# Experts' rows added to x2 in memory by the scatter, and a finish that loads one row per token

## The chip, the cores and the metric

One core of one Trainium2 chip runs the whole kernel. The metric is the time of one execution on the device in microseconds (us); it is the median of several runs. A profiled execution is a run of its own, with its own time.

## What is computed

One layer of a decoder on 1024 tokens of 1024 float32 values: a token mixer of three branches, then a mixture of experts, then a last RMS norm. The change is in the last two steps. In the reference's terms:

```python
x = x + hybrid_mixer(rms_norm(x, norm1_w), ...)          # the kernel calls this x2
h = rms_norm(x, norm2_w)                                  # h2
x = x + hierarchical_moe(h, ...)
return rms_norm(x, final_norm_w)
# hierarchical_moe: each token goes to 2 of 32 experts (both of one group), with weights
hid = silu(xblk @ w_gate[e]) * (xblk @ w_up[e])           # [rows, 512]
y   = hid @ w_down[e]                                     # [rows, 1024]
out[token] = weight_1 * y_first + weight_2 * y_second
```

So the result's row for a token is the norm of three rows added: x2 and two experts' weighted outputs.

## The kernel before

The kernel is a series of blocks with a barrier of all engines between them. Each engine has its own list of instructions and waits on semaphores. Behind each block `semaphores.clear` (line 57) lets POOL clear the block's semaphores and sets another barrier (line 58), in which every engine drains its queue.

`merge_and_route` finishes the mixer, stores x2 and h2 to memory (`s_x`, `s_h` in the profile's names), picks two experts for each token and stores a table: for each expert up to 128 records per slab with the token's number (column 0), the number of the pair, token + pick * 1024 (column 1), and the weight (column 2).

`experts_first_slabs` runs the 32 experts, one slab of at most 128 rows each. For each expert, float32 products are done as three products of split values: ACT copies a piece of weights of 128 x 2048 to a rounded `hi` (L2655, L2665), DVE takes the rest `lo` (L2710, L2715), and PE multiplies hi*hi, hi*lo and lo*hi (L2782, L2767). Who does what:

- SP loads the weights of the next expert: four pieces for gate and up (L2578) and two for down (L2590), 1 MB each, each when DVE has read the buffer's last content. Each piece has one buffer.
- POOL gathers the rows of h2 for expert e+2 (L2622) and then scatters the weighted outputs of expert e-1 (L2630). Before, a row goes to `pairs`, a scratch of 2048 rows in memory, at the number of its pair, so that each row is written once and nothing is read. The two indirect transfers share POOL's queue.
- ACT weighs the output (`weigh`, L2672) into one of two buffers `ye`, then POOL may scatter it. ACT waits until the scatter two experts back has landed.
- At the end of the block SP loads x2 back into SBUF: five pieces of 128 rows into `x2_kept` (L2599) during the last expert but one, three into buffers of down weights (L2603) when these are free, and the last norm's weights (L2604). Then it waits for all scatters (L2607), loads `todo`, the list of further slabs (L2608), and the pairs of the first four pieces of tokens (L2610), 1 MB each.

`experts_further_slabs` handles experts with more than 128 rows. Each engine reads `todo` and skips everything if it is empty, as with these inputs. SP first loads the pairs of the last four pieces (L2861); POOL clears a buffer (L2877).

`finish` takes the eight pieces of 128 tokens in turn. For the pieces 0, 1, 4 and 7 DVE adds the two rows of a pair (L3003) and adds that to x2 (L3005). For the pieces 2, 3, 5 and 6 PE adds the two rows by products with the identity into PSUM (L2988), and DVE makes the second addition alone. ACT takes the sum of squares (L3025), Ln (L3026) and Exp (L3027), DVE scales with the norm's weights (L3009), and SP stores the piece (L2978). DVE scales piece c-1 after it has added piece c.

Of the kernel before, what the change touches and what calls it, by code (L numbers as in the profile page):

```python
# [8 lines left out]
F32 = mybir.dt.float32  # L9
# [1748 lines left out]
GK, DK = 2 * KT // GU, FF // P // DN  # L1758
KEPT = 5
AHEAD = 2  # L1760
# [738 lines left out]

def experts_first_slabs(nc, io, dr, ident, dn_raw, gu_raw, x2_kept, x2_tail, final_w, recs, recs_in, todo, todo_in, pairs, pairs_in,  # L2500
                        kept_sem):
# [10 lines left out]
    with ExitStack() as ctx:  # L2512
# [24 lines left out]
        dn_used = sem("dn_used")  # L2537
        x2_in = sem("x2_in")
        gathered = [kept_sem(f"gathered{b}") for b in range(2)]
# [29 lines left out]
        def _(sp):  # L2569
# [27 lines left out]
            experts(body)  # L2597
            for c, kept in enumerate(x2_kept):
                sp.dma_start(kept[:], dr["x2"][c * CH:(c + 1) * CH, :]).then_inc(x2_in, 16)  # L2599
            sp.wait_ge(dn_ready, DN * LAST)  # L2600
            for n, tail in enumerate(x2_tail):
                c = len(x2_kept) + n
                sp.dma_start(tail, dr["x2"][c * CH:(c + 1) * CH, :]).then_inc(x2_in, 16)  # L2603
            sp.dma_start(final_w, io["final_norm_w"].unsqueeze(0).to_broadcast([P, D])).then_inc(x2_in, 16)  # L2604
            sp.wait_ge(dn_used, DN * N_EXPERTS)
            for b in range(2):
                sp.wait_ge(scattered[b], 16 * N_EXPERTS // 2)  # L2607
            sp.dma_start(todo[:], dr["work"].rearrange("(o n) w -> o (n w)", o=1)).then_inc(todo_in, 16)  # L2608
            for c in range(GU):
                sp.dma_start(pairs[c], pair_rows(dr, c)).then_inc(pairs_in[c], 16)  # L2610
            sp.wait_ge(x2_in, 16 * (NCH + 1))

        @block.gpsimd
        def _(pool):
# [11 lines left out]
            def scatter(e, b, turn):  # L2626

                pool.wait_ge(y_ready, e + 1)
                pool.sem_inc(passed, 1)
                pool.indirect_dma_start(out=dr["pairs"], out_offset=bass.IndirectOffsetOnAxis(ap=recs[:, e, 1:2], axis=0),  # L2630
                                        in_=ye[b][:], in_offset=None, bounds_check=2 * T - 1, oob_is_err=False)\
                    .then_inc(scattered[b], 16)
# [166 lines left out]

def pair_rows(dr, c):  # L2800

    return dr["pairs"].rearrange("(a t) d -> t a d", a=2)[c * CH:(c + 1) * CH]


def experts_further_slabs(nc, io, dr, ident, todo, todo_in, pairs, pairs_in):

# [3 lines left out]
    with ExitStack() as ctx:  # L2810
# [47 lines left out]
        @block.sync  # L2858
        def _(sp):
            for c in range(GU, NCH):  # L2860
                sp.dma_start(pairs[c], pair_rows(dr, c)).then_inc(pairs_in[c], 16)  # L2861
            sp.sem_inc(slab_done, 1)

            def body(n, place, expert):

                sp.wait_ge(slab_done, n + 1)
                one = bass.ds(expert, 1)
                sp.dma_start(rec[:].unsqueeze(1), dr["table"].rearrange("(s e) w -> s e w", e=N_EXPERTS)[bass.ds(place, SLAB), one, :])\
                    .then_inc(rec_in, 16)
                for w, p in ((wg, 0), (wu, GU // 2), (wdn, GU)):  # L2870
                    sp.dma_start(w[:].rearrange("p k f -> p (k f)").rearrange("p (a m) -> p a m", a=2),
                                 io["moe"][one, p:p + 2].rearrange("o a p m -> p (o a) m")).then_inc(w_in, 16)
            slabs(sp, body)

        @block.gpsimd
        def _(pool):
# [3 lines left out]
            def body(n, place, expert):  # L2880
# [6 lines left out]
                pool.sem_inc(passed, 1)  # L2887
                pool.indirect_dma_start(out=dr["pairs"], out_offset=bass.IndirectOffsetOnAxis(ap=rec[:, 1:2], axis=0),
                                        in_=ye[:], in_offset=None, bounds_check=2 * T - 1, oob_is_err=False)\
                    .then_inc(scattered, 16)  # L2890
# [3 lines left out]
            def first_load_past():  # L2894
                for c in range(NCH):
                    pool.wait_ge(pairs_in[c], 16)

            def load_again():
                for c in range(NCH):
                    pool.dma_start(pairs[c], pair_rows(dr, c)).then_inc(loaded_again, 16)  # L2900
                pool.wait_ge(loaded_again, 16 * NCH)
# [49 lines left out]

def finish(nc, out, ident, x2, final_w, pairs, pairs_in, kept_sems):

    ON_PE = (2, 3, 5, 6)
    with ExitStack() as ctx:
# [4 lines left out]
        cst = sb("fcst", [P, 1])  # L2962
        both = [ctx.enter_context(nc.psum_tensor(f"both{b}", [P, D], F32)) for b in range(len(ON_PE))]
        c_ready = sem("c_ready")
        both_ready = sem("both_ready")
        sum_ready = sem("sum_ready")
        rstd_ready = sem("rstd_ready")
        y_ready = sem("y_ready")
        stored = sem("stored")
        dve_own = sem("dve_own")  # L2970
        act_own = sem("act_own")
        block = ctx.enter_context(nc.Block())

        @block.sync
        def _(sp):
            for c in range(NCH):
                sp.wait_ge(y_ready, c + 1)
                sp.dma_start(out[c * CH:(c + 1) * CH, :], pairs[c][:, 1, :]).then_inc(stored, 16)  # L2978
            sp.wait_ge(stored, 16 * NCH)

        @block.tensor
        def _(pe):
            for n, c in enumerate(ON_PE):
                pe.wait_ge(pairs_in[c], 16)
                for half in range(2):
                    hs = slice(half * 512, half * 512 + 512)
                    for a in range(2):
                        ins = nc.tensor.matmul(both[n][:, hs], ident[:], pairs[c][:, a, hs], start=a == 0, stop=a == 1)  # L2988
                ins.then_inc(both_ready, 1)

        @block.vector
        def _(dve):
            own = Chain(dve, dve_own)
            nc.vector.memset(cst[:], EPS).then_inc(c_ready, 1)

            def add(c):
                if c in ON_PE:
                    n = ON_PE.index(c)
                    dve.wait_ge(both_ready, n + 1)
                    two = both[n][:]  # L3000
                else:
                    dve.wait_ge(pairs_in[c], 16)
                    own.link(nc.vector.tensor_tensor(pairs[c][:, 0, :], pairs[c][:, 0, :], pairs[c][:, 1, :], ALU.add))  # L3003
                    two = pairs[c][:, 0, :]
                nc.vector.tensor_tensor(x2[c], x2[c], two, ALU.add).then_inc(sum_ready, 1)  # L3005

            def scaled(c):
                dve.wait_ge(rstd_ready, c + 1)
                nc.vector.scalar_tensor_tensor(pairs[c][:, 1, :], x2[c], stat[:, c, 1:2], final_w, ALU.mult, ALU.mult)\  # L3009
                    .then_inc(y_ready, 1)  # L3010

            for c in range(NCH):
                add(c)
                if c >= 1:
                    scaled(c - 1)
            scaled(NCH - 1)

        @block.scalar
        def _(act):
# [3 lines left out]
            for c in range(NCH):  # L3023
                act.wait_ge(sum_ready, c + 1)
                own.link(nc.scalar.activation(sq[:], x2[c], ACT.Square, accum_out=stat[:, c, 0:1]))  # L3025
                own.link(nc.scalar.activation(stat[:, c, 0:1], stat[:, c, 0:1], ACT.Ln, scale=1.0 / D, bias=cst[:]))  # L3026
                nc.scalar.activation(stat[:, c, 1:2], stat[:, c, 0:1], ACT.Exp, scale=-0.5).then_inc(rstd_ready, 1)  # L3027


def build(nc, io, out):  # L3030
# [13 lines left out]
        ("table", [N_EXPERTS * T, 4], U32),  # L3044
        ("work", [16, 2], I32),
        ("pairs", [2 * T, D], F32))}
    with ExitStack() as ctx:
# [22 lines left out]
        def kept_sem(name):  # L3070
# [4 lines left out]
        todo_in = kept_sem("todo_in")  # L3075
        pairs_in = [kept_sem(f"pairs_in{c}") for c in range(NCH)]
        merge_and_route(nc, io, dr, ident, dn_raw, gate_raw, recs, recs_in, kept_sem)
        x2_kept = many(KEPT, "x2_kept", [P, D])
        x2_tail = [dn_raw[n // DK][:, n % DK, :] for n in range(NCH - KEPT)]
        final_w = dn_raw[DN - 1][:, DK - 1, :]  # L3080
        gu_raw = gate_raw + many(GU - AHEAD, "up_raw", [P, GK, FF])
        todo = ctx.enter_context(nc.sbuf_tensor("todo", [1, 2 * 16], I32, side="right"))
        pairs = [t[:].rearrange("p k f -> p (k f)").rearrange("p (a d) -> p a d", a=2) for t in gu_raw]
        experts_first_slabs(nc, io, dr, ident, dn_raw, gu_raw, x2_kept, x2_tail, final_w, recs, recs_in, todo, todo_in, pairs, pairs_in,
                            kept_sem)
        pairs += [t[:] for t in many(NCH - GU, "pairs", [P, 2, D])]
        experts_further_slabs(nc, io, dr, ident, todo, todo_in, pairs, pairs_in)
        finish(nc, out, ident, [kept[:] for kept in x2_kept] + x2_tail, final_w, pairs, pairs_in, kept_sems)

# [29 lines left out]
```

## Time and profile before

| | |
|---|---|
| Three runs | 2125.1, 2125.44, 2130.31 us, median 2125.44 |
| The profiled execution | 2123.97 us |
| Its span, first to last instruction | 2122.3 us |
| Mean granted TensorE clock | 0.965 |
| Busy: PE, DVE, ACT, POOL | 91%, 70%, 49%, 10% |
| DMA | 436.12 MB, 205 GB/s on average |

Times in the rows are us from the start of the span. PE is TensorE, DVE VectorE, ACT ScalarE, POOL GpSimd, SP SyncE; SPq and POOLq are an engine's queue instructions, a DMA's issue among them. `out<-in` are the tiles' names. An issue's own length is the time to give the transfer out, not the time to its landing.

### The profile page before, as it was taken

What the parts mean: (1) busy time and instruction counts of PE and PEld (TensorE: products, weight loads), DVE (VectorE), ACT (ScalarE), POOL (GpSimd) and SP (SyncE); (2) the same over time, 40 slices, a digit from 0 to 9 for tenths busy, and PEclk for the clock granted to TensorE, in tenths of its full rate; (3) what the DMA queues carried; (4) which work ended last, traced back from release to release, by engine and by line L of the source; (5) the groups of instructions that cost most, each with busy time, mean ns of one, the idle gap of its engine ahead of it and who ended that gap; (6) DMA issues with size and microseconds to landing.
All of it is one profiled execution on the core that took longest, in us unless ns stands there. A gap on an engine that the chain in (4) does not pass through costs nothing. (4 is left out here: it accounts for less than half of the span.)

```text
span 2122.3 us, 26908 instructions
## 1 busy us (share of the span) xinstructions
PE 1938.2 (91%) x10610; PEld 1585.1 (75%) x10611; DVE 1480.4 (70%) x1746; ACT 1049.7 (49%) x1235; POOL 213.5 (10%) x163
## 2 busy tenths in 40 slices
PE   6999999998879989899996998985799999999994
PEld 5789888887867767677774887874688888888872
DVE  5976676664126878878764565566799999999974
ACT  4324444453114544444544234331688888888863
POOL 2210000000020000000000000011122222222210
PEclk9999999999989999999998999997799999999997
DMA  5233223332163556646526654441899999999986
GB/s 162 84 137 100 94 96 129 100 119 100 60 154 120 155 142 171 166 127 137 158 94 254 225 203 169 173 175 59 327 371 384 386 388 383 389 387 386 384 325 249
DMA packets 212416, 436.12 MB, mean 205 GB/s; under 512 B 28018, under 2 KB 151042, under 8 KB 184770
## 3 DMA queue, kind: packets, MB, share of 16 engines
q1 hardware_dynamic: 180834, 361.97, 49.6%
q10 hardware_dynamic: 20576, 51.39, 6.8%
q0 software_dynamic: 10880, 21.03, 2.6%
q8 instruction: 85, 1.39, 0.3%
q14 instruction: 41, 0.34, 0.0%
HBM read 369.67 MB, written 81.43 MB: 213 GB/s over the span
## 5 line engine op out<-in xcount | busy, mean ns | idle before, releaser
L2710 DVE TENSOR_TENSOR gu_lo<-gate_raw,gu_hi 128x2048 fp32r<-128x2048 f32 x64 | 146.7, 2293 | 33.6 <-ACT gu_hi L2655 33.6
L1584 PE MATMUL psum<-h_hi,l_hi 128*128 128x512 f32 x384 | 158.8, 414 | 3.3 <-PEq L58 3.3
L1584 PE MATMUL psum<-h_lo,l_hi 128*128 128x512 f32 x384 | 159.8, 416 | 0.0
L1584 PE MATMUL psum<-h_hi,l_lo 128*128 128x512 f32 x384 | 156.9, 409 | 0.0
L2710 DVE TENSOR_TENSOR gu_lo<-up_raw,gu_hi 128x2048 fp32r<-128x2048 f32 x64 | 146.3, 2287 | 13.4 <-ACT gu_hi L2655 13.4
L2715 DVE TENSOR_TENSOR dn_lo<-dn_raw,dn_hi 128x2048 fp32r<-128x2048 f32 x62 | 142.0, 2292 | 17.0 <-ACT dn_hi L2665 13.0
L2665 ACT CAST dn_hi<-dn_raw 128x2048 fp32r<-128x2048 f32 x62 | 118.3, 1910 | 48.8 <-PE y_ps L2767 48.8
L2655 ACT CAST gu_hi<-up_raw 128x2048 fp32r<-128x2048 f32 x64 | 122.3, 1910 | 36.2 <-PE u_ps L2782 34.8
L2655 ACT CAST gu_hi<-gate_raw 128x2048 fp32r<-128x2048 f32 x64 | 122.5, 1915 | 34.1 <-PE g_ps L2782 34.1
L2423 PE MATMUL mpsum<-y_hi,wb_hi 128*128 128x512 f32 x256 | 104.0, 406 | 18.2 <-DVE y_lo L2178 14.0
L1240 ACT COPY l_out<-psum 128x512 f32<-128x512 f32 x48 | 28.1, 586 | 176.3 <-PE psum L1584 171.8
L2782 PE MATMUL g_ps<-gu_hi,xeT_hi 128*128 128x512 f32 x256 | 105.3, 411 | 5.5 <-DVE xeT_lo L2719 5.5
L803 DVE TENSOR_TENSOR w_lo<-w_raw,w_hi 128x512 fp32r<-128x512 f32 x90 | 61.7, 688 | 64.8 <-ACT w_hi L662 64.7
L2423 PE MATMUL mpsum<-y_hi,wb_lo 128*128 128x512 f32 x256 | 101.9, 398 | 0.0
L2423 PE MATMUL mpsum<-y_lo,wb_hi 128*128 128x512 f32 x256 | 101.9, 398 | 0.0
L2782 PE MATMUL g_ps<-gu_hi,xeT_lo 128*128 128x512 f32 x256 | 101.8, 398 | 0.0
L2782 PE MATMUL g_ps<-gu_lo,xeT_hi 128*128 128x512 f32 x256 | 101.6, 397 | 0.0
L662 ACT CAST w_hi<-w_raw 128x512 fp32r<-128x512 f32 x90 | 55.8, 622 | 90.7 <-PE ps L923 90.2
L2782 PE MATMUL u_ps<-gu_hi,xeT_lo 128*128 128x512 f32 x256 | 99.7, 389 | 0.0
L2782 PE MATMUL u_ps<-gu_hi,xeT_hi 128*128 128x512 f32 x256 | 99.6, 389 | 0.0
L2782 PE MATMUL u_ps<-gu_lo,xeT_hi 128*128 128x512 f32 x256 | 99.6, 389 | 0.0
L2068 ACT CAST wb_hi<-dn_raw 128x2048 fp32r<-128x2048 f32 x19 | 36.2, 1906 | 126.3 <-DMA dn_raw<-w_br 71.0
(439 smaller groups left out, 5229.8 us busy)
## 6 DMA issues: line engine op xcount, KB each, us to landing
gate_raw<-moe SPq DMA_DIRECT2D x66, 1024.0 KB, 8.8
up_raw<-moe SPq DMA_DIRECT2D x64, 1024.0 KB, 8.4
dn_raw<-moe SPq DMA_DIRECT2D x62, 1024.0 KB, 8.0
w_raw<-w_in SPq DMA_DIRECT2D x26, 1024.0 KB, 5.6
dn_raw<-w_br SPq DMA_DIRECT2D x15, 1024.0 KB, 7.2
l_raw<-w_gates ACTq DMA_DIRECT2D x24, 512.0 KB, 5.4
s_gates<-l_out ACTq DMA_DIRECT2D x48, 256.0 KB, 4.1
gate<-s_gates SPq DMA_DIRECT2D x16, 768.0 KB, 4.3
```

The costliest lines, as they stand in the source:

```text
L662: nc.scalar.copy(slot_hi[g], source(n, g)).then_inc(hi_ready, 1)
L803: ins = tt(slot_lo[g], source(n, g), slot_hi[g].bitcast(F32), ALU.subtract).then_inc(split_ready, 1)
L1240: nc.scalar.copy(l_out[h % 2][:], psum[:, late_bank(h), :]).then_inc(l_evicted, 1)
L1584: ins = nc.tensor.matmul(psum[:, bank, :], w[t % 2][:, k, :], x[:, k, half * 512:half * 512 + 512], start=i == 0, stop=i == LATE_MM - 1, s ...
L2068: nc.scalar.copy(out, w_raw[s % 2][:].rearrange("p k n -> p (k n)")).then_inc(w_hi_ready, 1)
L2423: ins = nc.tensor.matmul(ps[:, br, :], w[:, k * P:(k + 1) * P], y[:, k, :], start=k == k0 and q == 0, stop=k == k1 - 1 and q == 2)
L2655: nc.scalar.copy(gu_hi[p][:], gu_raw[p][:]).then_inc(gu_hi_ready, 1)
L2665: nc.scalar.copy(hi, raw).then_inc(dn_hi_ready, 1)
L2710: nc.vector.tensor_tensor(gu_lo[p][:], gu_raw[p][:], gu_hi[p][:].bitcast(F32), ALU.subtract).then_inc(gu_ready, 1)
L2715: nc.vector.tensor_tensor(lo, raw, hi.bitcast(F32), ALU.subtract).then_inc(dn_ready, 1)
L2782: ins = nc.tensor.matmul(ps[:], x[:, (p - at) * GK + k, :], w[:, k, :], start=p == at and k == 0 and q == 0, stop=p == at + GU // 2 - 1 an ...
```

## The change

The scatters, of the first and of the further slabs, go to x2 in memory at the token's number, with addition as the transfer's operation; each waits for the scatter before it to land. The scratch `pairs` is gone. SP no longer loads x2 ahead; after the last scatter it loads the eight pieces of x2, now complete, 512 KB each, in the first experts' block. `finish` squares and scales them in place; its additions on PE and DVE are gone. The computed result is the same but for the order of the additions.

```diff
 def experts_first_slabs(...):
             gate_up(0)
             experts(body)
-            for c, kept in enumerate(x2_kept):
-                sp.dma_start(kept[:], dr["x2"][c * CH:(c + 1) * CH, :]).then_inc(x2_in, 16)
             sp.wait_ge(dn_ready, DN * LAST)
-            for n, tail in enumerate(x2_tail):
-                c = len(x2_kept) + n
-                sp.dma_start(tail, dr["x2"][c * CH:(c + 1) * CH, :]).then_inc(x2_in, 16)
-            sp.dma_start(final_w, io["final_norm_w"].unsqueeze(0).to_broadcast([P, D])).then_inc(x2_in, 16)
+            sp.dma_start(final_w, io["final_norm_w"].unsqueeze(0).to_broadcast([P, D])).then_inc(final_in, 16)
             sp.wait_ge(dn_used, DN * N_EXPERTS)
             for b in range(2):
                 sp.wait_ge(scattered[b], 16 * N_EXPERTS // 2)
             sp.dma_start(todo[:], dr["work"].rearrange("(o n) w -> o (n w)", o=1)).then_inc(todo_in, 16)
-            for c in range(GU):
-                sp.dma_start(pairs[c], pair_rows(dr, c)).then_inc(pairs_in[c], 16)
-            sp.wait_ge(x2_in, 16 * (NCH + 1))
+            for c in range(NCH):
+                sp.dma_start(rows[c], dr["x2"][c * CH:(c + 1) * CH, :]).then_inc(rows_in[c], 16)
+            sp.wait_ge(final_in, 16)
...
             def scatter(e, b, turn):
                 pool.wait_ge(y_ready, e + 1)
+                if not first(e):
+                    pool.wait_ge(scattered[1 - b], 16 * ((e + 1) // 2))
                 pool.sem_inc(passed, 1)
-                pool.indirect_dma_start(out=dr["pairs"], out_offset=bass.IndirectOffsetOnAxis(ap=recs[:, e, 1:2], axis=0),
-                                        in_=ye[b][:], in_offset=None, bounds_check=2 * T - 1, oob_is_err=False)\
+                pool.indirect_dma_start(out=dr["x2"], out_offset=bass.IndirectOffsetOnAxis(ap=recs[:, e, 0:1], axis=0),
+                                        in_=ye[b][:], in_offset=None, bounds_check=T - 1, oob_is_err=False, compute_op=ALU.add)\
                     .then_inc(scattered[b], 16)
...
 def experts_further_slabs(...):
         def _(sp):
-            for c in range(GU, NCH):
-                sp.dma_start(pairs[c], pair_rows(dr, c)).then_inc(pairs_in[c], 16)
             sp.sem_inc(slab_done, 1)
...
 def finish(...):
         def _(sp):
             for c in range(NCH):
                 sp.wait_ge(y_ready, c + 1)
-                sp.dma_start(out[c * CH:(c + 1) * CH, :], pairs[c][:, 1, :]).then_inc(stored, 16)
+                sp.dma_start(out[c * CH:(c + 1) * CH, :], rows[c]).then_inc(stored, 16)
             sp.wait_ge(stored, 16 * NCH)
-        @block.tensor
...
         def _(dve):
             nc.vector.memset(cst[:], EPS).then_inc(c_ready, 1)
-            def add(c):
...
-            for c in range(NCH):
-                add(c)
-                if c >= 1:
-                    scaled(c - 1)
-            scaled(NCH - 1)
+            for c in range(NCH):
+                dve.wait_ge(rstd_ready, c + 1)
+                nc.vector.scalar_tensor_tensor(rows[c], rows[c], stat[:, c, 1:2], final_w, ALU.mult, ALU.mult).then_inc(y_ready, 1)
...
             for c in range(NCH):
-                act.wait_ge(sum_ready, c + 1)
-                own.link(nc.scalar.activation(sq[:], x2[c], ACT.Square, accum_out=stat[:, c, 0:1]))
+                act.wait_ge(rows_in[c], 16)
+                own.link(nc.scalar.activation(sq[:], rows[c], ACT.Square, accum_out=stat[:, c, 0:1]))
```

The rows lie in the four buffers of gate and up weights, two pieces in each; the five buffers `x2_kept` and the four of `pairs` in SBUF are gone.

## Rows read from the trace of the kernel before

**Rows 1.** The page's slices: GB/s that DMA moved in 40 equal parts of the span.

```profile
GB/s 162 84 137 100 94 96 129 100 119 100 60 154 120 155 142 171 166 127 137 158 94 254 225 203 169 173 175 59 327 371 384 386 388 383 389 387 386 384 325 249
```

**Rows 2.** Busy time by stretch; the last three columns are clock, DMA share, GB/s.

```profile
1600.00:2000.00 400.00, 400.00 (x1899) 332.47 (x1898) 361.18 (x204) 321.80 (x227) 94.91 (x44) 1.00 1.00 387
1809.15:1826.88 17.73, 17.73 (x86) 14.73 (x85) 15.99 (x9) 14.26 (x11) 4.32 (x3) 1.00 0.99 397
2083.00:2088.00 5.00, 0.00 (x0) 0.00 (x0) 0.00 (x0) 0.00 (x0) 0.00 (x0) 0.50 1.02 416
```

**Rows 3.** Timeline of POOL, 1800 to 1845: start, length, engine, line, operation, idle before.

```profile
1805.37 1.32 POOL L2630 DMA_INDIRECT s_pairs<-ye,recs  x1 [13.12 <-ACT ye L2672]
1806.99 3.00 POOL L2622 DMA_INDIRECT xe<-s_h,recs  x1 [0.30 <-issue]
1823.10 1.32 POOL L2630 DMA_INDIRECT s_pairs<-ye,recs  x1 [13.11 <-ACT ye L2672]
```

**Rows 4.** Timeline of ACT, the same stretch.

```profile
1816.57 1.91 ACT L2665 CAST dn_hi<-dn_raw 128x2048 fp32r<-128x2048 f32 x1 [0.81 <-PE y_ps L2767]
...
1822.58 1.92 ACT L2655 CAST gu_hi<-gate_raw 128x2048 fp32r<-128x2048 f32 x1
...
1827.94 1.91 ACT L2655 CAST gu_hi<-up_raw 128x2048 fp32r<-128x2048 f32 x1 [0.31 <-PE u_ps L2782]
```

**Rows 5.** Timeline of SP's issues, the same stretch, then landing times of L2578's loads.

```profile
1809.12 2.96 SPq L2578 DMA_DIRECT2D gate_raw<-moe  x2
1814.48 3.13 SPq L2578 DMA_DIRECT2D up_raw<-moe  x2
...
DMA to landing us min/median/max: 4.6/8.6/9.6
```

**Rows 6.** The last scatter; landings of the 32 scatters (L2630), of the 32 gathers (L2622).

```profile
2076.70 0.97 POOL L2630 DMA_INDIRECT s_pairs<-ye,recs  x1 [7.16 <-ACT ye L2672]
...
DMA to landing us min/median/max: 3.2/8.9/9.5
...
DMA to landing us min/median/max: 5.8/11.2/11.9
```

**Rows 7.** Timeline of SP's issues from 2080.

```profile
2080.31 0.89 SPq L2610 DMA_DIRECT2D gate_raw<-s_pairs  x2
2081.24 1.23 SPq L2610 DMA_DIRECT2D up_raw<-s_pairs  x2
2088.82 1.91 SPq L2861 DMA_DIRECT2D pairs<-s_pairs  x4
```

**Rows 8.** POOL's next instruction, and line 58's drains of POOL's queue (ns min/median/max).

```profile
2088.83 0.95 POOL L2877 MEMSET xxe<- 128x1024 f32 x1 [11.15 <-POOLq L58]
...
L58 POOLq DRAIN  x7: 34/41/5282, 135.3 to 2122.0; - x7
```

**Rows 9.** Timeline of ACT from 2088, the first piece of `finish`.

```profile
2092.49 1.28 ACT L3021 ACT_TABLE_LOAD   x1 [2.38 <-PEq L58]
2095.15 1.06 ACT L3025 ACTIVATE fsq<-x_kept 128x1024 f32<-128x1024 f32 x1 [1.37 <-DVE x_kept L3005]
...
2096.65 0.20 ACT L3027 ACTIVATE fstat<-fstat 128x1 f32<-128x1 f32 x1
```

**Rows 10.** Timeline of DVE, the last scaling.

```profile
2117.23 1.28 DVE L3009 SCALAR_TENSOR_TENSOR pairs<-dn_raw,fstat 128x1024 f32<-128x1024 f32 x1 [0.58 <-ACT fstat L3027]
```

**Rows 11.** The page's DMA queues: packets, MB, share of 16 engines; POOL's is q0.

```profile
q0 software_dynamic: 10880, 21.03, 2.6%
```

**Rows 12.** The page's and the DMA view's issues: count, KB each, median us to landing.

```profile
wmat<-s_b_ssm SPq DMA_DIRECT2D x8, 1024.0 KB, 16.6
...
gate_raw<-s_pairs SPq DMA_DIRECT2D x2, 1024.0 KB, 6.3
```

**Rows 13.** POOL's DMA queue from 2070 on.

```profile
q0 software_dynamic: 288, 0.61, 3.0%
```

**Rows 14.** The five loads of x2 at L2599: ns min/median/max, first and last start.

```profile
L2599 SPq DMA_DIRECT2D x_kept<-s_x x5: 432/433/711, 2042.7 to 2044.6; - x5
```

More of the change, by code:

```diff
@@ L1758 @@
 GK, DK = 2 * KT // GU, FF // P // DN
-KEPT = 5
 AHEAD = 2
@@ L2497, in _, with experts_first_slabs @@
             nc.tensor.matmul(cnt_ps, ones[:], cnt[:], start=True, stop=True).then_inc(cnt_ready, 1)
-def experts_first_slabs(nc, io, dr, ident, dn_raw, gu_raw, x2_kept, x2_tail, final_w, recs, recs_in, todo, todo_in, pairs, pairs_in,
+def experts_first_slabs(nc, io, dr, ident, dn_raw, gu_raw, final_w, recs, recs_in, todo, todo_in, rows, rows_in,
                         kept_sem):
@@ L2537, in experts_first_slabs @@
         dn_used = sem("dn_used")
-        x2_in = sem("x2_in")
+        final_in = sem("final_in")
         gathered = [kept_sem(f"gathered{b}") for b in range(2)]
@@ L2797, in _, with experts_further_slabs @@
             down(LAST)
-def pair_rows(dr, c):
-    return dr["pairs"].rearrange("(a t) d -> t a d", a=2)[c * CH:(c + 1) * CH]
-def experts_further_slabs(nc, io, dr, ident, todo, todo_in, pairs, pairs_in):
+def experts_further_slabs(nc, io, dr, ident, todo, todo_in, rows, rows_in):
     FK = FF // P
@@ L2887, in body @@
                 pool.sem_inc(passed, 1)
-                pool.indirect_dma_start(out=dr["pairs"], out_offset=bass.IndirectOffsetOnAxis(ap=rec[:, 1:2], axis=0),
-                                        in_=ye[:], in_offset=None, bounds_check=2 * T - 1, oob_is_err=False)\
+                pool.indirect_dma_start(out=dr["x2"], out_offset=bass.IndirectOffsetOnAxis(ap=rec[:, 0:1], axis=0),
+                                        in_=ye[:], in_offset=None, bounds_check=T - 1, oob_is_err=False, compute_op=ALU.add)\
                     .then_inc(scattered, 16)
@@ L2895, in first_load_past @@
                 for c in range(NCH):
-                    pool.wait_ge(pairs_in[c], 16)
+                    pool.wait_ge(rows_in[c], 16)
             def load_again():
                 for c in range(NCH):
-                    pool.dma_start(pairs[c], pair_rows(dr, c)).then_inc(loaded_again, 16)
+                    pool.dma_start(rows[c], dr["x2"][c * CH:(c + 1) * CH, :]).then_inc(loaded_again, 16)
                 pool.wait_ge(loaded_again, 16 * NCH)
@@ L2949, in _, with finish @@
             slabs(pe, body)
-def finish(nc, out, ident, x2, final_w, pairs, pairs_in, kept_sems):
-    ON_PE = (2, 3, 5, 6)
+def finish(nc, out, rows, final_w, rows_in, kept_sems):
     with ExitStack() as ctx:
@@ L2962, in finish @@
         cst = sb("fcst", [P, 1])
-        both = [ctx.enter_context(nc.psum_tensor(f"both{b}", [P, D], F32)) for b in range(len(ON_PE))]
         c_ready = sem("c_ready")
-        both_ready = sem("both_ready")
-        sum_ready = sem("sum_ready")
         rstd_ready = sem("rstd_ready")
@@ L2969, in finish @@
         stored = sem("stored")
-        dve_own = sem("dve_own")
         act_own = sem("act_own")
@@ L2977, in _ @@
                 sp.wait_ge(y_ready, c + 1)
-                sp.dma_start(out[c * CH:(c + 1) * CH, :], pairs[c][:, 1, :]).then_inc(stored, 16)
+                sp.dma_start(out[c * CH:(c + 1) * CH, :], rows[c]).then_inc(stored, 16)
             sp.wait_ge(stored, 16 * NCH)
-        @block.tensor
[L2982 to L2989, printed above, removed]
         @block.vector
         def _(dve):
-            own = Chain(dve, dve_own)
             nc.vector.memset(cst[:], EPS).then_inc(c_ready, 1)
-            def add(c):
[L2997 to L3007, printed above, removed]
-                dve.wait_ge(rstd_ready, c + 1)
-                nc.vector.scalar_tensor_tensor(pairs[c][:, 1, :], x2[c], stat[:, c, 1:2], final_w, ALU.mult, ALU.mult)\
-                    .then_inc(y_ready, 1)
-            for c in range(NCH):
-                add(c)
-                if c >= 1:
-                    scaled(c - 1)
-            scaled(NCH - 1)
+            for c in range(NCH):
+                dve.wait_ge(rstd_ready, c + 1)
+                nc.vector.scalar_tensor_tensor(rows[c], rows[c], stat[:, c, 1:2], final_w, ALU.mult, ALU.mult).then_inc(y_ready, 1)
         @block.scalar
@@ L3044, in build @@
         ("table", [N_EXPERTS * T, 4], U32),
-        ("work", [16, 2], I32),
-        ("pairs", [2 * T, D], F32))}
+        ("work", [16, 2], I32))}
     with ExitStack() as ctx:
@@ L3075, in build @@
         todo_in = kept_sem("todo_in")
-        pairs_in = [kept_sem(f"pairs_in{c}") for c in range(NCH)]
+        rows_in = [kept_sem(f"rows_in{c}") for c in range(NCH)]
         merge_and_route(nc, io, dr, ident, dn_raw, gate_raw, recs, recs_in, kept_sem)
-        x2_kept = many(KEPT, "x2_kept", [P, D])
-        x2_tail = [dn_raw[n // DK][:, n % DK, :] for n in range(NCH - KEPT)]
         final_w = dn_raw[DN - 1][:, DK - 1, :]
@@ L3082, in build @@
         todo = ctx.enter_context(nc.sbuf_tensor("todo", [1, 2 * 16], I32, side="right"))
-        pairs = [t[:].rearrange("p k f -> p (k f)").rearrange("p (a d) -> p a d", a=2) for t in gu_raw]
-        experts_first_slabs(nc, io, dr, ident, dn_raw, gu_raw, x2_kept, x2_tail, final_w, recs, recs_in, todo, todo_in, pairs, pairs_in,
+        rows = [gu_raw[c // 2][:].rearrange("p k f -> p (k f)")[:, c % 2 * D:c % 2 * D + D] for c in range(NCH)]
+        experts_first_slabs(nc, io, dr, ident, dn_raw, gu_raw, final_w, recs, recs_in, todo, todo_in, rows, rows_in,
                             kept_sem)
-        pairs += [t[:] for t in many(NCH - GU, "pairs", [P, 2, D])]
-        experts_further_slabs(nc, io, dr, ident, todo, todo_in, pairs, pairs_in)
-        finish(nc, out, ident, [kept[:] for kept in x2_kept] + x2_tail, final_w, pairs, pairs_in, kept_sems)
+        experts_further_slabs(nc, io, dr, ident, todo, todo_in, rows, rows_in)
+        finish(nc, out, rows, final_w, rows_in, kept_sems)
 def kernel(**inputs):
```

## The prediction

> **What bounds the kernel now.** I read the page's slices first [rows 1]. The expert stage stands out: from about 1540 to 2015 us memory traffic is at 371 to 389 GB/s, above everything before. The busy times of that stretch [rows 2] say what is full: PE is busy for all of the 400 us, at a granted clock of 1.00, and the DMA share is 1.00 too. Two resources are nearly full, so the next question is which one waits for the other. The scatter's starts are 17.73 us apart, time after time [rows 3]. ACT's copies of the weights wait for PE to give back a buffer ("<-PE y_ps", "<-PE u_ps"), not for a load [rows 4], while SP issues six loads of 1 MB for each expert at fixed places of the period [rows 5]. A gate piece issued at 1809.12 lands some 8.6 us later, at 1817.7, and is copied at 1822.58: 4.9 us of margin; the `up` piece issued at 1814.48 lands at 1823.1 and is copied at 1827.94, a margin of 4.8 us. So PE sets the period, and DMA sits just below it. The change adds work to DMA, and that margin is what has to cover it.
>
> Then the end of the kernel, from the last scatter on. It is issued at 2076.70 and lands after 3.2 us [rows 6]; no other engine has work left then, and SP waits for that landing before it loads anything. SP issues four loads of pairs to 2082.47 [rows 7]; no engine starts again before 2088.83 [rows 8], and the gap is a DRAIN of POOL's queue at the barrier, 5.28 us at its longest of seven [rows 8]. The block of the further slabs finds no work: SP issues four more loads (to 2090.73) and `finish` begins at 2092.49 [rows 7, 9]. In `finish` DVE is busy nearly throughout, to 2118.51 [rows 10]: eight pieces, each two additions or one, and a scaling. That is 26.0 us. From the last scaling's end to the span's end are 3.8 us, the last store.
>
> **The change, part by part.** The sum is made against the profiled execution, 2123.97 us with a span of 2122.3; the median of the runs is 2125.44, 1.5 above it.
>
> *In the expert stage.* PE, ACT and DVE do the same. What changes is the scatter's transfer. 1024 tokens by two picks are 2048 rows, 64 for an average expert. Before, a row of 4 KB is read from SBUF and written to memory; now the old row of x2 must be read too. Queue q0's 2.6% of 16 engines over 2122.3 us are 883 engine-us for 21.03 MB [rows 11], or 0.17 us for 4 KB. The trace has no adding transfer. The lower bound is nothing extra. The far end is the slowest large transfer of the page, `wmat<-s_b_ssm`, 1024 KB in 16.6 us [rows 12], 63 GB/s: 64 rows (0.26 MB) at that rate are 4.2 us. I take one more read of the row, since this is a whole row of 4 KB like its plain neighbour's: 64 x 0.17 / 16 = 0.7 us of DMA per expert.
>
> Is it hidden? The stage moves 387 GB/s [rows 2], 6.86 MB in 17.73 us. Where loads alone are queued, at 2083 to 2088, the same engines move 416 GB/s [rows 2], so one expert's bytes need 16.5 us and 1.2 us are free. 0.7 fits. It would stop fitting at 1.2 us per expert, that is at 0.30 us more for each row, or 1.8 extra packets. I cost this part at nothing; its cover is the 1.2 us and, for a crowded expert, the 4.8 us of a load's margin. Without cover it is the first rival.
>
> What speaks against it is a limit stated elsewhere. First the rows: they show 397 GB/s over one whole period and 416 in the tail [rows 2]. The Trainium skill (DMA: Bandwidth & Descriptors, Specifications) sets a core's share of memory at about 358 GB/s, under a fabric ceiling of 435. By the 358 the stage would already stand at its limit and the whole extra read would be paid, 0.26 MB / 358 GB/s = 0.73 us x 31 = 23 us slower, an estimate from that page; the trace, at 397, is above that limit and near the other. On the price of a row the Trainium skill (Collectives: The Full Stack, The bandwidth ceiling) says that an adding transfer reads two sources through one ring and runs at half the rate of a copy; by that the stage's sum is the same as mine, and no row here shows it.
>
> *The scatter's new wait.* Scatter e waits until scatter e-1 has landed. That one was issued 17.73 us earlier and lands in 8.9 [rows 3, 6]: 8.8 us early, at no cost. Behind it on POOL is the gather for expert e+3, which starts 1.6 us after the scatter [rows 3], lands in 11.2 [rows 6] and is used about a period later still; an adding scatter that took 8 us more would delay nobody. The same holds for `ye`, which ACT writes again two experts later.
>
> *The loads of x2 for the last expert* (five at L2599, three at L2603, 4 MB) go away under PE's work of experts 30 and 31. PE did not wait for DMA there: 0. The final weights' load stays.
>
> *The last scatter* is on the path. The low end is 3.2 us as before; the high end the 8.9 us which scatters take in the full stage, 5.7 more. Nothing else is queued here, so I stay near the low end: q0 moved 0.61 MB for the two last scatters [rows 13], 0.30 MB or 74 rows each, five per engine at 0.17 us = 0.8 more, with a little for the longer round trip: **+1.0**.
>
> *SP's issues before the barrier* are eight of 512 KB instead of four of 1 MB. Four took 2.16 us [rows 7]; five of the new size start within 1.9 us (2042.7 to 2044.6), 0.48 each [rows 14], so eight take 3.8: **+1.7**, as the drain starts when SP arrives. The drain I leave at 5.28 us; the low end is 0.03, the shortest of the row, the high end I can't bound by a row above 5.28.
>
> *The block of further slabs.* SP issued to 2090.73 and `finish` began 1.76 us later. Without these loads POOL's memset is last, 2088.83 + 0.95 = 2089.78 [rows 8]: **-0.95**.
>
> *finish.* PE's 32 matmuls, DVE's twelve additions and ACT's waits for them go. ACT becomes the chain: Square at 2095.15, then Ln, then Exp at 2096.65 for 0.20 [rows 9], 1.72 us with the gap. The start is its table load, 1.28 us. Then 8 x 1.72 = 13.8 and DVE's last scaling 1.28 with 0.03 before it: 16.4 instead of 26.0, **-9.6**. DVE's scaling (1.28 per piece) and the stores (0.33 to issue) fit within 1.72. Are the rows there? They are 4 MB, 10.1 us at 416 GB/s. The first issue is at 2081.3, the first load of pairs took some 2.8 us besides its transfer (6.3 for the median of two in a row [rows 12]), so the last row lands near 2094.2, while ACT begins at 2095.5 and asks for piece 7 another 12 us on. No wait. The store at the end stays 3.8.
>
> Sum: 1.0 + 1.7 - 0.95 - 9.6 = -7.85 us. The profiled execution would be 2116.1, the median 2117.6.
>
> **The rivals.**
> A. *The adding scatter fills DMA* (slower). Place: SP's loads in the stage; decides from 1.8 extra packets per row. For it: the DMA share of 0.99 to 1.00 for 500 us [rows 2], which leaves little idle time in any engine. Against: the fixed 17.73 us, the loads' margin, the 416 GB/s. At three extra packets a row costs 0.51 us, 2.0 us per expert, 0.8 over the cover; over some 28 experts, once the margin of 4.8 us is used up, +22 us: 2140. At the far end, 4.2 us, it is 3.0 x 30 = 90 us: 2208. Chance 0.19.
> B. *The tail gives most back* (no measurable change). The last scatter takes as long as those of the full stage, 4.7 more than I take, and nothing in the tail can hide it, for SP waits for it alone: -3.1, 2122.3. The same comes of a drain that grows with the longer transfer before it. For it: the drain's 5.28 us are not explained by any row. Against: the last scatter now meets empty queues. Chance 0.24.
> C. *The drain shrinks*, its time being counted from the last scatter, or set by loads that now are fewer: 2112 to 2115, inside the forecast's side. Chance 0.07.
> That the change does not do what it says: the rows of one scatter are different tokens, and the wait keeps two scatters apart, so all the additions are made; I see no case for that.
>
> **How the numbers follow.** About 0.3% (6.4 us) is what a measurement of this kernel can tell from no change. The forecast, 2117.6, has 0.50; its own spread (scatter +0 to +3, drain some us either way) puts 0.06 of that above 2119.1. Faster: 0.44 + 0.07 = 0.51. Same: 0.06 + 0.24 = 0.30. Slower: 0.19. The range starts at 2112.0 (scatter at no extra, -1.0, and most of the drain gone, -4.6) and ends at 2129.0, past B and the mildest form of A; it leaves out most of A and some of C.
>
> **What would show it.** Right: scatters still 17.73 us apart; their landing somewhat over 8.9 us; the last one lands in about 4.2; `finish` 16.4 us long with ACT's Squares 1.72 apart and no wait for a load; POOL's drain near 5.3. Wrong: PE or ACT waiting for `gate_raw` or `dn_raw` loads (A); a last scatter of 8 us or a drain above 8 (B); Squares that wait for rows. The forecast as a whole fails if the expert stage gets longer by over 8 us.

## The result, and the profile after

The changed kernel takes 2143.55 us against 2126.0 for the kernel before in the same measurement: a ratio of 1.0079, 95% interval 1.0053 to 1.0105, slower by about 17 us. The forecast was 2117.6 in a range of 2112.0 to 2129.0. The profiled execution of the changed kernel has a span of 2143.5 us, 21.2 more than before: 1.2 ahead of the first scatter, 26.9 from the first scatter to the last, and 6.8 less behind the last.

Its slices of GB/s and its queue of indirect transfers, beside [rows 1] and [rows 11]:

```profile
GB/s 160 89 130 99 84 104 128 99 122 95 60 152 134 142 150 162 163 158 139 139 85 270 234 182 172 218 106 151 311 376 375 356 364 361 361 363 362 358 303 168
...
q0 software_dynamic: 10880, 21.03, 3.6%
```

The stage that moved 384 to 389 GB/s now moves 356 to 364. The same 21.03 MB of q0 take 3.6% of the engines' span instead of 2.6%: 0.036 x 16 x 2143.5 = 1235 engine-us (the busy times of the 16 engines added up) against 883, so 352 more, or 0.69 us for each expert when divided by 16 engines and 32 experts. That is the price that the prediction had put on it. Busy time by stretch, the same columns as [rows 2]:

```profile
1600.00:2000.00 400.00, 383.15 (x1792) 315.27 (x1791) 338.21 (x193) 300.19 (x213) 90.62 (x42) 1.00 0.98 363
```

PE is now idle for 16.85 of 400 us. The waits name what is late (engine, tile, line, whom it waited for: us in total, times, longest), over the expert stage and what follows it:

```profile
ACT dn_hi L2661 <- DMA dn_raw<-moe: 71.6, 47, 2.2
ACT gu_hi L2651 <- DMA up_raw<-moe: 37.8, 24, 2.1
PE g_ps L2778 <- DVE xeT_lo L2715: 25.7, 22, 2.8
```

ACT, which before waited for PE [rows 4], waits for loads of weights. The low parts that DVE makes and PE's products follow it. The loads' landings (count, KB each, median us), where [rows 5] had 8.6:

```profile
gate_raw<-moe SPq DMA_DIRECT2D x66, 1024.0 KB, 13.8
up_raw<-moe SPq DMA_DIRECT2D x64, 1024.0 KB, 14.3
dn_raw<-moe SPq DMA_DIRECT2D x62, 1024.0 KB, 14.5
```

And POOL's timeline, beside [rows 3]:

```profile
1895.24 1.88 POOL L2626 DMA_INDIRECT s_x<-ye,recs  x1 [13.98 <-ACT ye L2668]
1897.42 2.45 POOL L2616 DMA_INDIRECT xe<-s_h,recs  x1 [0.30 <-issue]
1914.11 1.87 POOL L2626 DMA_INDIRECT s_x<-ye,recs  x1 [14.23 <-ACT ye L2668]
```

The scatters are 18.9 us apart here, not 17.73. The first five distances are still 17.7 to 17.9, the sixth is 18.6 and from then on they lie around 18.9, between 18.2 and 19.8, until the last two experts. This is the picture of a margin of the loads that is used up first, after which each expert pays. From the first scatter to the last it is 564.2 us, 26.9 more than the 537.3 of before.

The end of the kernel, in the landings of the 32 scatters (L2626) and the timelines of POOL, SP, ACT and DVE, beside [rows 6], [rows 7], [rows 9] and [rows 10]:

```profile
DMA to landing us min/median/max: 6.1/10.7/11.6
...
2104.77 1.57 POOL L2626 DMA_INDIRECT s_x<-ye,recs  x1 [6.58 <-ACT ye L2668]
2121.58 0.95 POOL L2866 MEMSET xxe<- 128x1024 f32 x1 [15.25 <-POOLq L58]
...
2111.06 0.29 SPq L2602 DMA_DIRECT2D todo<-s_work  x1
2111.39 1.77 SPq L2604 DMA_DIRECT2D gate_raw<-s_x  x4
2113.20 2.02 SPq L2604 DMA_DIRECT2D up_raw<-s_x  x4
...
2124.28 1.28 ACT L2974 ACT_TABLE_LOAD   x1 [1.42 <-PEq L58]
2125.57 1.06 ACT L2978 ACTIVATE fsq<-gate_raw 128x1024 f32<-128x1024 f32 x1
...
2127.19 1.04 ACT L2978 ACTIVATE fsq<-gate_raw 128x1024 f32<-128x1024 f32 x1
...
2138.52 1.28 DVE L2969 SCALAR_TENSOR_TENSOR up_raw<-up_raw,fstat,dn_raw 128x1024 f32<-128x1024 f32 x1 [0.32 <-ACT fstat L2980]
```

From the last scatter's issue to the end of the span it is 38.8 us instead of 45.6: 6.8 us gained. So the tail did nearly what was forecast, and the stage lost four times as much.

### The profile page after: what moved, and what is told of

The parts are those of the page before. It is cut to its first block and busy times, and to the rows that moved or that the text cites. A ratio compares the mean times of both kernels' runs of the same rounds, so it can differ in the third digit from the quotient of the medians.

```text
span 2143.5 us, 26824 instructions
## 1 busy us (share of the span) xinstructions
PE 1930.6 (90%) x10578; PEld 1580.7 (74%) x10579; DVE 1465.2 (68%) x1734; ACT 1045.8 (49%) x1235; POOL 213.4 (10%) x163
## 3 DMA queue, kind: packets, MB, share of 16 engines
q0 software_dynamic: 10880, 21.03, 3.6%
## 5 line engine op out<-in xcount | busy, mean ns | idle before, releaser
L2626 POOL DMA_INDIRECT s_x<-ye,recs x32 | 59.2, 1851 | 456.6 <-ACT ye L2668 456.6
```

The costliest lines, as they stand in the source:

```text
L2626: pool.indirect_dma_start(out=dr["x2"], out_offset=bass.IndirectOffsetOnAxis(ap=recs[:, e, 0:1], axis=0), in_=ye[b][:], in_offset=None, bo ...
```

## The experiments

Three theories could explain the stage. **Theory 1**: the rows of an expert lie in the first of 128 partitions and are carried by only some of the 16 DMA engines; the fullest of these became slower than PE. **Theory 2**: all 16 engines, or the memory, are full. **Theory 3**: the new wait holds POOL. Before the runs I read from the trace's records when each load's 16 completion marks came, one from each engine that carried a share of it. Medians over 150 to 480 us after the first scatter, in us from issue, for the pieces of `up`:

```
mark                 1st   8th  12th  15th  16th
kernel before        5.4   6.5   7.5   8.0   8.5
changed kernel       5.9   6.6   9.6  13.5  14.5
```

Half the engines are done as early as before, the others lag. That is what theory 1 says. The Trainium skill (DMA: Bandwidth & Descriptors, The descriptor swizzle) gives, for a transfer to 128 partitions, partitions 0 to 63 to engines 0 to 7, by (partition / 4) mod 8, and the upper ones to engines 8 to 15; the marks, eight early and eight late, agree with it, and the edits below were made by it. By this rule and the reference's routing, which gives the experts 38 to 107 rows, the fullest engine has eight rows with every expert, and the upper eight engines have rows only of experts with over 64.

**The rows spread over the engines.** Same bytes, same additions; only the place of an expert's records changes.

```diff
-            sp.dma_start(recs[:], dr["table"].rearrange("(s e) w -> s e w", e=N_EXPERTS)[0:SLAB]).then_inc(recs_in, 16)
+            for a in range(4):
+                sp.dma_start(recs[a::4], dr["table"].rearrange("(s e) w -> s e w", e=N_EXPERTS)[a * 32:a * 32 + 32]).then_inc(recs_in, 16)
```

(and 64 for 16 in the two waits for `recs_in`).

> The changed kernel, only that an expert's records are put into every part of the 128 partitions: record r goes to partition 4*(r mod 32) + r/32, so that an expert of some 64 rows no longer keeps them in the lower 64 partitions. Bytes, rows and additions stay the same. Theory 1 (some DMA engines carry all the rows, and the period of the slowest engine became longer than PE's): scatters 17.7 us apart again, weights land in under 9 us instead of 14, about 27 us less than the changed kernel, 2116 us, 10 less than the kernel before. Theory 2 (all 16 DMA engines or the memory are full with the extra read): same bytes, so still 18.9 us apart and 2143 us.

Measured: a ratio to the kernel before of 0.9984 (0.9969 to 0.9999). Its stretch, its scatters and its landings:

```profile
1600.00:2000.00 400.00, 400.00 (x1898) 332.34 (x1897) 360.98 (x204) 321.31 (x226) 96.47 (x45) 1.00 1.01 386
...
1880.62 1.87 POOL L2627 DMA_INDIRECT s_x<-ye,recs  x1 [13.12 <-ACT ye L2669]
1882.80 2.45 POOL L2617 DMA_INDIRECT xe<-s_h,recs  x1 [0.30 <-issue]
1898.35 1.87 POOL L2627 DMA_INDIRECT s_x<-ye,recs  x1 [13.11 <-ACT ye L2669]
...
up_raw<-moe SPq DMA_DIRECT2D x64, 1024.0 KB, 7.8
...
ACT dn_hi L2662 <- PE y_ps L2764: 49.0, 60, 0.8
```

PE is busy for all 400 us, the scatters are 17.73 us apart, ACT waits for PE again, and the stage takes 539.0 us, 25.3 less than the changed kernel's. Theory 2 fails: the bytes are the same. The time came down by some 3 us and not by the 10 that I had expected, which rested on a single profile of either kernel. In this profile the tail is 7.9 us shorter than in the kernel before and the stage 1.6 longer, but the first scatter comes 4.3 us later, at 1543.7, and 3.7 of these are already there when `merge_and_route` begins, in code that no edit touches. That part ends between 1133.5 and 1148.7 us over all the profiles of this case, and no run tells why. The two repetitions below say how much the whole gains.

**The same spreading in the kernel before.**

> The kernel before with the same spreading of the records. Theory 1: PE sets the period in both, so the scatters stay 17.73 us apart and the time stays at 2126 us (the three further small loads of records cost up to 1 us), but the loads of weights land in 5 to 7 us instead of 8.6, and the scatters and gathers earlier. Theory 2: landing times as before, 8.6 us.

Measured: 1.0018 (1.0005 to 1.003), 17.73 us apart as before, and the loads land earlier:

```profile
up_raw<-moe SPq DMA_DIRECT2D x64, 1024.0 KB, 6.3
dn_raw<-moe SPq DMA_DIRECT2D x62, 1024.0 KB, 5.9
```

As expected, a margin that nobody needed grew by 2 us. The loss, some 4 us, is more than the 1 us that I had allowed for the further loads of records. The block that makes them, `merge_and_route`, takes 348.2 to 349.5 us in the six profiles with spread records and 345.9 to 348.1 in the eight others, so some 1.8 us of it are there; the rest is not explained.

**The wait alone, in the kernel before.**

```diff
                 pool.wait_ge(y_ready, e + 1)
+                if not first(e):
+                    pool.wait_ge(scattered[1 - b], 16 * ((e + 1) // 2))
```

> The kernel before with the wait of each scatter for the one before it, and nothing else of the change. If the wait has no part in the loss: 2126 us as before, scatters 17.73 us apart. Theory 3 (the wait holds POOL, the gathers behind it and with them PE): up to 27 us slower.

Measured: 0.9997 (0.9983 to 1.0012), and 17.69 us between scatters:

```profile
1880.90 1.29 POOL L2632 DMA_INDIRECT s_pairs<-ye,recs  x1 [13.11 <-ACT ye L2674]
...
1898.59 1.30 POOL L2632 DMA_INDIRECT s_pairs<-ye,recs  x1 [13.09 <-ACT ye L2674]
```

Theory 3 falls: the wait is free. In the changed kernel an adding scatter lands after 11.6 us at most (see above), still well before the next one is due.

**The change without the addition.**

```diff
-                                        in_=ye[b][:], in_offset=None, bounds_check=T - 1, oob_is_err=False, compute_op=ALU.add)\
+                                        in_=ye[b][:], in_offset=None, bounds_check=T - 1, oob_is_err=False)\
```

> The changed kernel with a scatter that writes its rows over those of x2 and does not add (the sums of the result are left out). Everything else of the change is there, the wait, the loads and the short finish. Theories 1 and 2 both: without the second read the period is 17.73 us again, and the time 2114 to 2117 us: 27 us come back in the stage and some 2 to 3 us in the last scatter, which lands in 3.2 us again instead of 6.1. Theory 3: the period stays at 18.9 us.

Measured: 2118.75 us, just above the range given, beside 2128.75 for the kernel before: a ratio of 0.9955 (0.9939 to 0.997). The stage takes 537.8 us, the tail 35.7, 3.1 less than the changed kernel's, and the last scatter lands after 3.2 us again. The queue's share is back as well:

```profile
q0 software_dynamic: 10880, 21.03, 2.6%
...
2081.34 0.97 POOL L2626 DMA_INDIRECT s_x<-ye,recs  x1 [8.78 <-ACT ye L2668]
```

This gives the price of the addition at both places: 26.4 us in the stage, 3.1 in the tail. The trace's records of single packets say how it arises. Mean and percentiles of q0's packets of 4 KB over 400 us of the stage, in ns (gathers and scatters together):

```
                 mean   5%  25%  50%  75%  99%
kernel before     160  159  159  159  159  166
changed kernel    242  159  159  159  327  328
```

Nearly half the packets now take twice as long; half of all are the scatter's, and nothing else of them has changed. The Trainium skill (Collectives: The Full Stack, The bandwidth ceiling) says that an adding transfer reads both sources through one ring and runs at half the rate; 328 against 159 ns agrees.

**Extra rows without any addition.** If it is the fullest engine, a third plain transfer of the same rows must cost as much as the addition. The writing kernel was given one:

```diff
+                if e >= 2:
+                    wait_past(pool, spare_in, 16 * (e - 2))
+                    pool.sem_inc(passed, 1)
+                    pool.indirect_dma_start(out=spare[:], out_offset=None, in_=dr["h2"],
+                                            in_offset=bass.IndirectOffsetOnAxis(ap=recs[:, e, 0:1], axis=0),
+                                            bounds_check=T - 1, oob_is_err=False).then_inc(spare_in, 16)
```

> No addition in any transfer: the kernel whose scatter writes over x2 (the sums of the result are left out), and POOL gathers each expert's rows of h2 once more into a spare buffer that nobody reads, from the third expert on. Theory 1 (the lower 64 partitions' DMA engines): an engine has its 48 packets of weights at 0.309 us, 14.8 us, and eight rows three times at 0.16 us, together 18.7 us, as much as in the changed kernel. So the scatters are 18.5 to 19 us apart, the stage is 25 to 30 us longer than the 538 us of the writing kernel, and the weights land in about 14 us. If an addition in the transfer were slow by more than its second packet: less than 5 us longer.

> The same with the third transfer of rows, but with the records spread over all the partitions (4*(r mod 32) + r/32). Same bytes. Theory 1: 14.8 + 3 x 4.7 x 0.16 = 17.1 us for the fullest engine, under PE's 17.7, so the scatters are 17.7 us apart and the stage takes 538 to 540 us. Theory 2 (all engines full): as long as the run without the spreading.

(4.7 is the fullest engine's number of rows with this spreading, a mean over the 32 experts, counted from the reference's routing.) Measured: a stage of 563.4 us, ratio 1.0098 (1.0079 to 1.0116), without the spreading; 539.0 us, ratio 0.9968 (0.9952 to 0.9984), with it. Stretch and landing of the first, then of the second:

```profile
1600.00:2000.00 400.00, 385.34 (x1804) 317.00 (x1803) 342.23 (x193) 304.74 (x216) 135.79 (x66) 1.00 0.99 380
...
dn_raw<-moe SPq DMA_DIRECT2D x62, 1024.0 KB, 14.4
```

```profile
1600.00:2000.00 400.00, 400.00 (x1898) 332.33 (x1897) 360.98 (x205) 320.98 (x226) 148.86 (x68) 1.00 1.01 402
...
dn_raw<-moe SPq DMA_DIRECT2D x62, 1024.0 KB, 7.0
```

The same bytes: 380 GB/s and PE starved in one, 402 GB/s and PE full in the other. The 25 us have nothing to do with adding as such, nor with a limit of the memory at 387 GB/s. What the runs do not tell apart is whether an engine itself is full or the path between it and its partitions; for a forecast it comes to the same.

**A plain load of as many bytes.** SP loads 64 rows of h2 per expert, shared by all engines.

```diff
+                if not last(e):
+                    wait_past(sp, spare_in, 16 * e)
+                    sp.dma_start(spare[0:64, :], dr["h2"][0:64, :]).then_inc(spare_in, 16)
```

> The writing kernel (the sums of the result are left out), and SP loads 64 whole rows of h2 (256 KB, as much as an average gather) into a spare buffer once per expert, a plain load that all 16 engines share. Same bytes as the extra gather. Theory 1: four rows at 0.16 us come to every engine, so the fullest has 14.8 + 2 x 8 x 0.16 + 0.6 = 18.0 us: 17.9 to 18.1 us apart, the stage 5 to 12 us longer than 538. Theory 2: as slow as with the extra gather, 25 to 30 us longer.

Measured: 2178.54 us, ratio 1.0216 (1.0196 to 1.0235), a stage of 597.1 us, 59 more than without the load. Neither theory said that. The 15th completion mark of an `up` piece comes after 8.1 us, the 16th after 15.5: one single engine is late. Two runs followed.

> The writing kernel (the sums of the result are left out) with spread records and the plain load of 64 rows per expert, which without the spreading made the stage 59 us longer instead of 5 to 12. By theory 1 alone the fullest engine has 14.8 + 4.7 x 0.32 + 0.6 = 16.9 us: 17.7 us apart and 538 us. If the plain load itself costs one engine more than its four rows (theory 4), one engine still lands the weights in over 10 us and the stage stays over 550 us.

> The writing kernel (the sums of the result are left out) with the plain load, records not spread, the load taking 64 other rows of h2 for each expert instead of the same ones. If it was the repeated reading of the same addresses that stretched the packets: the stage 5 to 12 us over 538. If not: some 59 us over it as before.

Measured: with spread records a stage of 574.3 us, ratio 1.014 (1.0093 to 1.0187); with other rows each time (`dr["h2"][e % 16 * 64:e % 16 * 64 + 64, :]`) 595.2 us, ratio 1.0235 (1.0183 to 1.0286). So repeated addresses are not the cause. Spreading takes back 23 of the 59 us, which I put down to theory 1; 36 us stay with the plain load itself, on one or two engines (marks with spreading: 12th after 8.4 us, 16th after 15.2). Why such a load costs an engine more than four rows at 0.16 us is open, and it shows that adding up packets, as theory 1 does, can be far too low for a plain load of 64 partitions. It does not bear on the change, which has no such load, but it warns against adding small plain loads to this stage.

**The best version, twice more**, the second time beside the changed kernel on one chip.

> The changed kernel with the records spread, once more and in more rounds. In the profile its stage was 25 us shorter than the changed kernel's and its end 8 us shorter than that of the kernel before: 6 to 8 us less than the kernel before, a ratio of 0.996 to 0.998.

> The changed kernel itself, on the same chip and against the same runs of the kernel before as the next ones: 17 to 20 us over the kernel before, a ratio of 1.008, the scatters 18.9 us apart from the sixth on, the weights landing in 14 us.

> The changed kernel with spread records, beside the changed kernel on one chip: 6 to 9 us under the kernel before, and 24 to 28 us under the changed kernel.

Measured: spread 0.9958 (0.9942 to 0.9974); then, against the same runs of the kernel before, the changed kernel 1.0101 (1.0065 to 1.0136) and the spread one 0.9971 (0.9952 to 0.9989). Medians of the last pair are 2148.05 and 2121.45 us. These are 21 us over the kernel before, where 17 to 20 were expected, and 6 under it, as expected. The changed kernel's stretch and then the spread one's, same chip:

```profile
1600.00:2000.00 400.00, 382.15 (x1795) 314.90 (x1794) 337.87 (x192) 299.54 (x213) 91.60 (x43) 1.00 0.98 362
```

```profile
1600.00:2000.00 400.00, 400.00 (x1895) 332.29 (x1894) 360.61 (x203) 321.44 (x227) 99.23 (x46) 1.00 1.01 385
```

The change with four lines beside it is the fastest kernel that computes the whole result: 3 to 9 us under the kernel before over the three measurements (0.9984, 0.9958, 0.9971), and 27 us under the change alone.

## Why the prediction was wrong

**The step that failed** is "Is it hidden?": the cover of 1.2 us per expert. The other factor, the load on it, was right: "one more read of the row", 0.7 us of DMA per expert, came out as 0.69. The cover was worked out for the 16 engines as one pool, from 416 GB/s against 387. But a gather or scatter puts the rows where the records lie, in the first partitions, and so mostly on half of the engines. For the fullest of them an estimate from the packets' durations: 768 packets of weights at 0.309 us over 16 engines are 14.8 us, gather and scatter of eight rows each at 0.16 are 2.6, together 17.4 of the 17.73 us. Only 0.3 us were free. The addition puts eight more reads there at 0.17 = 1.4 us, which makes 18.8; 18.9 was measured. The sum takes the median duration of a weights' packet; with the mean, 0.336, it would be over 17.73 for the kernel before already. So the runs show that the fullest engine decides, and the 0.3 us are no more than an estimate. By it the point of decision was not 1.8 extra packets per row but about a quarter of one.

So rival A came true with the wrong condition. Its place (SP's loads) and its look (ACT waiting for loads, of `dn_raw` and `up_raw`; for `gate_raw` it waited only once) were right. That its time, 2140, came near 2143.55 is luck: it charged three extra packets, 0.8 us over the cover per expert, where one packet cost 1.2. Its chance of 0.19 rested on "at three extra packets", and one was enough. I had put the share of 1.00 in [rows 2] on its side and the full-rate stretch against it. Both were averages over engines; the stretch at 416 GB/s was made of plain loads of whole pieces. The 358 GB/s of the Trainium skill (DMA: Bandwidth & Descriptors, Specifications), which I had weighed, were rightly not taken as a limit: 402 GB/s were sustained with PE full. Yet the loss that this rule gave, 23 us, came near the 26.9 measured, for a reason that it does not contain.

The steps of the tail, in the order of the prediction:

- *The last scatter*, forecast +1.0: it lands 6.2 us after its issue at 2104.77, against 3.2 before, and SP goes on at 2111.06. This is **+3.0**, the term that was mis-sized in the tail. POOL's instruction itself takes 1.57 us instead of 0.97, which I had left out. The second read I had put at five rows per engine, the same mean over 16 engines as in the stage; eight rows are 1.3 us. The rest, about 1, no row explains. Spreading helps here too: 5.1 to 5.4 us in three profiles.
- *SP's issues*, +1.7: from 2111.39 to 2115.22 are 3.83 us instead of 2.16. Right.
- *The drain*, unchanged: 2115.22 to 2121.58 are 6.36 us, exactly as from 2082.47 to 2088.83. Rival C rested on it and fell. Rival B rested on it or on a last scatter of 8.9 us; the scatter went half that way, and the tail as a whole still gained 6.8 us. I had left the drain alone because I could not explain it, so its part of the forecast was right without a reason. The runs have one: its length follows the number of transfers that POOL gave out in the block. With none it is 34 to 41 ns at L58, with 24 (`merge_and_route`) 2.02 us, with 64 (the experts) 5.28, and with the 94 of the two runs with a third transfer of rows 7.73: some 82 ns for each. The change leaves their number at 64.
- *The block of further slabs*, -0.95: 2.70 us instead of 3.66. Right.
- *finish*, -9.6: from 2124.28 to 2139.80 are 15.5 us against 26.0, -10.5. ACT's period is 1.60 and not 1.72, since the next Square begins before Exp's record ends (2127.19 against 2127.28). It waits for no row.

Together -6.8, where -7.85 was forecast. The new wait and the removed loads of x2 cost nothing, as said: the wait was tried alone, and the kernel without the addition, which has both, takes 537.8 us for the stage against 537.3. One reading was off without harm: the gather behind scatter e is that for expert e+4, not e+3.

## What to carry to other kernels

Before you hide a transfer under a full DMA stage, work out the load of the fullest engine and not the mean: a gather or scatter that uses a part of its partitions uses a part of the engines. The times of the 16 completion marks of one load show this at once. Where rows fill only part of a slab, spreading the records over the partitions costs some small loads and can give back what the stage lost. An adding scatter is fine where the engines have room for a second read of each row, and its last one stands in the open with some 3 us more.

## What the runs showed of the hardware

- A DMA share of 1.00 over 400 us did not mean that the engines were full: with spread records the kernel moved a third transfer of rows, 402 GB/s instead of 385, at the same share and the same period. Weights' packets average 336 ns in the kernel before with a median of 309, and 325 with spread rows and one more transfer, so part of what is recorded as busy seems to be waiting.
- An adding packet of 4 KB takes 328 ns against 159 for a plain one. POOL gives out an adding scatter in 1.57 us against 0.97 when nothing else runs, and lands it 3 us later.
- The drain of POOL's queue at the barrier behind a block takes some 82 ns for each transfer that POOL gave out in the block. Behind the experts' block it is 5282 ns in every run with 64 of them, and 7732 ns in the two runs with 94, here the one with spread records:

```profile
L58 POOLq DRAIN  x7: 34/41/7732, 134.9 to 2120.5; - x7
```

- A plain load of 64 rows of 4 KB per expert made one engine late by some 7 us and the stage 59 us longer; no run here explains it.
